# Rows of the twelve small experts gathered as halves of 2 KB into 128 partitions instead of 4 KB into 64

## The reference

```python
probs = jax.nn.softmax(jnp.dot(t, w_router).astype(jnp.float32), axis=-1)
...
h = jax.nn.silu(jnp.einsum("td,edf->tef", t, w_gate)) * jnp.einsum("td,edf->tef", t, w_up)
h = h * gates.astype(h.dtype)[..., None]
return jnp.einsum("tef,efd->td", h, w_down).reshape(B, L, D)
```

## Time and profile before

| | us |
|---|---|
| median of 3 runs | 646.52 (644.9 to 649.55) |
| span of the profiled execution | 643.7 |
| end of the last weight load in it | 613.9 |

### The profile page before, as it was taken

One profiled execution on the slowest core, in us unless ns is written; L12 is line 12 of the kernel. 1 busy time (PEld: TensorE's weight loads), 2 busy tenths in 40 slices (PEclk: granted clock), 3 DMA queues, 4 the chain that ended last, 5 costly groups with the idle time before them and its releaser, 6 DMA issues.

```text
span 643.7 us, 13218 instructions
## 1 busy us (share of the span) xinstructions
PE 562.1 (87%) x5746; PEld 369.7 (57%) x5746; DVE 245.1 (38%) x532; ACT 138.8 (22%) x265; POOL 66.0 (10%) x99
## 2 busy tenths in 40 slices
PE   2789999999999899879998899999997667688664
PEld 0475553566675655764465799998554434354332
DVE  2562457986854844631076821111110000001125
ACT  1240444423216710210034021001010000000012
POOL 1039000000004000002011010000010000100131
PEclk9898999999999999989999999999999988999968
DMA  8989920113030560999949899999999999999962
GB/s 271 392 299 370 347 104 28 63 69 131 1 130 9 208 252 1 339 330 245 400 159 381 322 326 390 386 384 395 363 389 392 391 387 394 392 408 408 356 227 98
DMA packets 80139, 175.98 MB, mean 273 GB/s; under 512 B 6504, under 2 KB 11631, under 8 KB 79695
## 3 DMA queue, kind: packets, MB, share of 16 engines
q1 hardware_dynamic: 65808, 149.02, 63.4%
q0 software_dynamic: 5920, 18.36, 8.1%
q10 hardware_dynamic: 8351, 7.73, 3.7%
HBM read 162.62 MB, written 12.47 MB: 272 GB/s over the span
## 4 chain that ended last, share of the span: by engine, by line
PE 24%; SPq 21%; DMA 4%; DVE 4%; issue 2%; ACT 0%; DVEq 0%
SPq L1155 9%; PE psum L927 5%; PE psum L825 5%; DMA slot<-in_w_down 4%; PE psum L924 4%; SPq L1168 3%; SPq L1184 2%; PE psum L935 2%; SPq L1225 2%; PE psum L832 2%; SPq L1172 2%; SPq L1181 1%; PE psum L841 1%; PE psum L1100 1%; PE psum L485 1%
## 5 line engine op out<-in xcount | busy, mean ns | idle before, releaser
L573 PE MATMUL psum<-hT,slot 128*128 128x384 f32 x304 | 100.8, 489 | 0.0
L935 PE MATMUL psum<-slot,xeTa 128*32 128x256 f32 x1152 | 69.2, 394 | 18.4 <-DMA slot<-in_w_gate 9.3
L573 PEld LDWEIGHTS psum<-hT,slot 128*128 128x128 f32 x304 | 56.9, 190 | 38.2
L935 PEld LDWEIGHTS psum<-slot,xeTa 128*32 128x32 f32 x1152 | 42.1, 113 | 44.7 <-issue 15.1
L582 PE MATMUL psum<-slot,hT 128*128 128x512 f32 x96 | 42.3, 595 | 1.2 <-DMA slot<-in_w_in 1.2
L935 PE MATMUL psum<-slot,heT 128*32 128x256 f32 x576 | 35.4, 401 | 8.6 <-DMA slot<-in_w_down 8.5
L1680 ACT ACTIVATE he<-psum 128x256 f32<-128x256 f32 (+1 forms) x16 | 6.6, 411 | 141.5 <-PE psum L935 113.0
L2363 DVE TENSOR_TENSOR he<-he,psum 128x256 f32<-128x256 f32 (+1 forms) x16 | 7.3, 454 | 73.0 <-PE psum L935 55.2
L2367 DVE COPY heT<-psum 128x256 f32<-128x256 f32 (+1 forms) x16 | 7.3, 458 | 70.8 <-PE psum L955 70.8
L924 PE MATMUL psum<-slot,xeTa 128*32 128x384 f32 x288 | 32.8, 487 | 0.3 <-issue 0.3
L927 PE MATMUL psum<-slot,xeTa 128*32 128x128 f32 x288 | 33.0, 273 | 0.0
(11 more groups left out here) (476 smaller groups left out, 912.1 us busy)
## 6 DMA issues: line engine op xcount, KB each, us to landing
slot<-in_w_ada SPq DMA_DIRECT2D x12, 2048.0 KB, 13.0
slot<-in_w_gate SPq DMA_DIRECT2D x12, 2048.0 KB, 17.5
slot<-in_w_up SPq DMA_DIRECT2D x12, 2048.0 KB, 18.3
slot<-in_w_down SPq DMA_DIRECT2D x12, 2048.0 KB, 19.5
slot<-in_w_in SPq DMA_DIRECT2D x7, 2048.0 KB, 11.3
const<-in_w_gate SPq DMA_DIRECT2D x4, 1792.0 KB
y_rows<-T POOLq DMA_DIRECT2D x11, 384.0 KB, 15.4
slot<-in_w_out SPq DMA_DIRECT2D x2, 2048.0 KB, 15.6
```

The costliest lines, as they stand in the source:

```text
L573: last = mm(o[:, 0:TOK], w[:, kt, tile(i)], hT[:, kt, :], start=(kt == 0), stop=(kt == KT - 1))
L935: last = mm(psum[32 * c:32 * c + 32, bank, 0:HALF], x(k, c % 2), w(k)[:, c // 2 * HALF:c // 2 * HALF + HALF], start=(k == 0), stop=(k == t ...
```

## The change

For the small experts the source of the gather is seen as 768 rows of 2 KB. Partition p below 64 fetches the first half of token row p, partition p from 64 on the second half of token row p - 64. Four transposes of 128 by 128 then fill the same bank of PSUM; block order in `xeTs` becomes 0, 4, 1, 5, 2, 6, 3, 7, and `up` reads it by that order. The doubled lists are made by one matmul with a new constant `twice` at the start of `expert(2)` on PE, and by an addition of 1 for the upper 64 partitions on DVE ahead of its work for expert 2. POOL waits for them ahead of the gather of n = 4 (before, it had them together with the list of n = 2). The two new constants, 129 columns, stand ahead of `dft_ctx` in `const`, and move all that lies behind them.

```diff
     put("triu", (p[:, None] < p[None]).astype(float))
+    put("twice", 2.0 * (p[:, None] == p[None] % SMALL))
+    put("upper", (p >= SMALL).astype(float)[:, None])
...
                 if small(n):
-                    for kt in range(KT):
-                        c = kt * SMALL
-                        last = tr(psum[:, 0, c:c + SMALL], src[0:SMALL, tile(kt)], ident[0:SMALL, 0:SMALL])
+                    for kt in range(KT // 2):
+                        last = tr(psum[:, 0, tile(kt)], src[:, tile(kt)], ident)
                     return last
...
                 if small(n):
-                    return packed_small(bank, lambda k, g: xeTs[p][:, k, 32 * g:32 * g + 32], lambda k: w[k], KT)
+                    return packed_small(bank, lambda k, g: xeTs[p][:, 2 * (k % 4) + k // 4, 32 * g:32 * g + 32],
+                                        lambda k: w[k], KT)
...
                 w = weights(n, 1)
+                if n == 2:
+                    pe.wait_ge(s["lists"], 1)
+                    mm(psum[:, 7, 32:32 + E - NBIG], C("twice"), OV[:, 10, NBIG:E], start=True, stop=True,
+                       skip_group_check=True).then_inc(s["sel_used"], 1)
...
                     if n + 1 == E - 1:
-                        pe.wait_ge(s["lists"], 2)
+                        pe.wait_ge(s["lists"], 3)
...
                 elif n == 2:
                     pool.wait_ge(s["lists"], 1)
+                elif n == NBIG:
+                    pool.wait_ge(s["lists"], 2)
...
-                m = SMALL if small(n) else ROWS
-                g.indirect_dma_start(out=xe[n % 2][0:m, :], out_offset=None, in_=A["h2_rows"],
-                                     in_offset=bass.IndirectOffsetOnAxis(ap=lst[0:m, n:n + 1], axis=0)
+                if small(n):
+                    to, of, by = xe[n % 2][:, 0:CW], A["h2_rows"].rearrange("t (h c) -> (t h) c", h=2), lst[:, n:n + 1]
+                else:
+                    to, of, by = xe[n % 2][0:ROWS, :], A["h2_rows"], lst[0:ROWS, n:n + 1]
+                g.indirect_dma_start(out=to, out_offset=None, in_=of, in_offset=bass.IndirectOffsetOnAxis(ap=by, axis=0)
                                      ).then_inc(s[f"xe{n % 2}"], 16)
...
-            v.tensor_copy(lst[:, 2:E], OV[:, 10, 2:E]).then_inc(s["lists"], 1)
+            v.tensor_copy(lst[:, 2:NBIG], OV[:, 10, 2:NBIG]).then_inc(s["lists"], 1)
...
-            def experts(it, first, last_pair=False):
+            def experts(it, first, last_pair=False, halves=False):
                 for p in range(2):
                     n = 2 * it + p
+                    if halves and p == 0:
+                        dve.wait_ge(s["sel_used"], NT + 1)
+                        v.tensor_scalar(lst[:, NBIG:E], psum[:, 7, 32:32 + E - NBIG], C("upper"), None, ALU.add
+                                        ).then_inc(s["lists"], 1)
...
-            experts(1, False)
+            experts(1, False, halves=True)
...
-            dve.wait_ge(s["sel_used"], NT + 1)
+            dve.wait_ge(s["sel_used"], NT + 2)
```

## The result

| | before | after |
|---|---|---|
| median of the runs, us | 647.06 (644.9 to 649.55, 4 runs) | 637.1 (636.43 to 638.13, 4 runs) |
| ratio, 95% interval | | 0.9865 [0.9828, 0.9901] |
| span of the profiled execution, us | 643.7 | 636.3 |
| last weight load issued and landed, us | 586.35, 613.9 | 578.02, 604.97 |

The change makes the kernel 1.35% faster, about 8.7 us by the ratio (6.4 to 11.1 us by its interval). The direction and the mechanism hold; the size does not.

A forecast was written before the change was run, and what follows sets the result against it. The DMA engines, not PE, were taken to bound the end of the experts. Terms -5.5 + 0.5 + 0 + 0 + 0.1 + 0.2 = -4.7 us gave a span of 639.0, a median of 641.8 us, range 638.5 to 648.0.

The forecast's parts named there:

- What bounds the kernel: End of the experts: set by the DMA engines, all 16 busy; PE time is not scarce; last weight load lands at 613.9.
- The loss: Behind each small gather the DMA rate drops from 404 to 347 GB/s: 0.64 us each, 7.6 us for twelve.
- half-rate reasoning: Small gather into partitions 0 to 63: at 202 GB/s per half it needs 1.30 us, 0.65 us more.
- Step 1: Small gathers into 128 partitions: 0.18 us of loss stays in each, gain 0.46 each, 5.5 us for twelve.
- Step 2: Twice the packets in the small gathers, on the DMA path: costs 0.04 us each, 0.5 us for twelve.
- Step 3: Four transposes instead of eight on PE: 0.69 us against 0.71, worth nothing on the time.
- Step 4: Late lists and POOL's wait for them: gather of n = 4 issued at 406.4, 2.7 us of cover, costs nothing.
- Step 5: Moved constants: longer load of `const` costs 0.1 us, gate matrix's new destination 0.2 us (bounds nothing and 4.6).
- Rival A: Small gathers: the loss goes altogether, being a matter of which half of the partitions is written; 639.6 us, chance 0.25.
- B: Small gathers: the loss stays, coming from fetching rows by a list in whatever partitions; 647.3 us, chance 0.20.
- C: Small gathers: the loss grows with the number of packets, holding up weight packets; 655 us, chance 0.08.
- D: Loads into `const`: packets to the moved destination take longer; gain gone at 4.7 us, or 657 us; chance 0.05.

The follow-up runs named there:

- e4_no_gather: Kernel before with the twelve small experts' gathers left out, a plain load of 1 KB in place of each: ratio 0.9755 to the kernel before.
- e8_eight: Changed kernel with eight products of 64 columns in place of the four transposes of 128: 638.04 us, ratio 0.9864 to the kernel before.
- e2_low: Control for e1_middle: same matmuls, constant and late lists, but the 64 whole rows land in partitions 0 to 63: ratio 0.9996 to the kernel before.
- e7_const_end: Changed kernel with its two new constants at the end of their table: 636.72 us, ratio 0.9849 to the kernel before.
- e1_middle: Kernel before with the 64 whole rows gathered into partitions 32 to 95, turned by selection matmuls, lists made late: ratio 0.9881.
- e3_halves_low: Kernel before with rows cut in 2 KB halves, two gathers of 64 halves, both into partitions 0 to 63: ratio 1.0022.
- e10_two_pieces: As e1_middle, but two gathers of 32 whole rows, into partitions 0 to 31 and 64 to 95: ratio 1.0005 to the kernel before.
- e6_spread4: As e1_middle, but four gathers of 16 whole rows, from partitions 0, 16, 64 and 80 on: 665.84 us, ratio 1.0306 to the kernel before.
- e12_quarters: Changed kernel with each small expert's rows in two gathers of 128 quarters of 1 KB into all 128 partitions: ratio 0.9917 to the kernel before.

## Why the prediction was wrong

**What bounds the kernel: right.** The DMA engines set the end: they finish 8.9 us earlier, and the slower tail takes 1.5 us of that back. The strip was read too evenly, though: DMA shows 8 and not 9 in slice 22, and PE has two slices of 8 among its 6 and 7 behind 480 us. The reading does not hang on it. PE is busy 11.60 of 16.00 us from 496 to 512 us, where it was 10.68, and waits for weights in the rest.

**The loss: right, a little small.** 12 * 0.64 = 7.6 us was called all that the change can win. The stretches of 4.5 us give 54 * (1 - 347/405.8) = 7.8 us with the rates of the two traces, the account with e4_no_gather 8.0. The half-rate reasoning (12 * 0.65 = 7.8 us) fits all three.

**Step 1: wrong, and it is the main term.** This is the step that failed. It took -5.5 us where -7.8 was measured, because it left a rest of 0.18 us of the loss in each gather where the rates show none. The residual of 0.18 us came from the closing gather, whose packets take 189 ns against 160 ns undisturbed, and by that ratio a 128-partition gather would have kept over half of the loss. In the kernel after, the small gather's own 64 packets take 10.6 us, 165 ns each with its 16 small ones counted to them. That is nearly the undisturbed time. So the 189 ns belonged to the tail and not to the form of the gather; what makes them long there was not tried. The row was the only one with 128 partitions, but not from the same situation.

**Step 2: wrong.** +0.5 us was for twice the packets; there are as many as before, 80140 against 80139. There was a row to doubt it by: nothing in the earlier trace rows says that one piece of the list is one packet, since 80 packets stood for 64 rows.

**Step 3: right.** Nothing that can be measured on the time, as e8_eight shows. Four transposes take 0.60 us, where 0.69 was worked out and eight took 0.71. All engines of the kernel after in order of time, around 416 us:

```profile
416.58 0.60 PE L946 MATMUL psum<-const,xe 128*128 128x128 f32 x4
```

**Step 4: right.** The gathers of n = 4 and 5 were put at 406.4 and 407.6. POOL, kernel after, in order of time, answers to the earlier trace rows:

```profile
406.00 0.99 POOL L1365 DMA_INDIRECT xe<-h_rows,lst  x1 [32.30 <-DVE lst L2372]
407.30 0.97 POOL L1365 DMA_INDIRECT xe<-h_rows,lst  x1 [0.30 <-issue]
```

PE turned the rows of n = 4 at 416.58, as before at 416.28, without a stop. e2_low has the same late lists at a ratio of 0.9996.

**Step 5: no cost is seen.** +0.3 us was taken. The loads into `const` run at 396 and 397 GB/s after, 389 before, and at 393 from 509.5 to 514 us in e7_const_end, which has the old destination. So the rates show no cost; the time of e7_const_end is too coarse to tell 0.3 us from nothing.

**The sum.** With -7.8, 0, 0, 0 and 0 it would have been 638.7 us. The median is 637.1, the ratio gives 637.8 (635.4 to 640.1). In the pair of traces the last load lands at 604.97 (near 609 was forecast), 8.9 us earlier, of which 0.4 was there before the first small gather and 0.6 is the load itself (26.95 against 27.53 us). These are of the size of the scatter between executions. That leaves nothing over that the runs could put a name to.

**The rivals and the range.** Rival A, the loss goes altogether, is what happened, in its reason too: it was given 0.25. What was held against it was the 96-row gathers, with a loss of 0.76 us each where halves explain 0.32. That number came from one stretch of one execution, and it is a poor one: the same stretch, 376 to 382.5, with the same code behind it, shows 310 before, 333 after, 301 in e7_const_end and 280 in e8_eight. It still loses more than halves explain in all of them, and why stays open; but it is no ground to expect a rest of the loss in the small gathers. B fell with the rates of 406. C fell with e1_middle, which has 80 packets a gather as before and no loss; the change itself does not test C, since its packets did not become more. D fell with the 396 and 397 GB/s of the loads into `const` (under 350 would have shown it) and with e7_const_end. The low end of the range was 1 us below rival A, and A had been charged with the 0.5 and 0.3 us of steps 2 and 5 as if these were sure, though step 5 itself had nothing as a bound and no row showed a cost for step 2. With them at nothing, A is at 638.8, and a margin below it of half the spread of the runs (4.7 us over the three of before) in place of the 1 us would have taken 637.1 in.

## What to carry to other kernels

When the DMA engines bound a kernel and the rate dips while their share stays at 1.0, look at which partitions the small transfers beside the stream are written to. One gather of 262 KB into partitions 0 to 63 halved the rate of all transfers together while it lasted, and put into 32 to 95 or into all 128 it cost only its bytes. The balance had to hold within each gather, because the gathers of POOL's queue were served one after the other (two valleys in e3_halves_low and e10_two_pieces, four in e6_spread4), so prefer one wide gather to several narrow ones. And when a cause is supported by a number that fits (0.65 against 0.64 us), a doubt that rests on a single short stretch should first be tested on how much that stretch scatters.

## What was not expected of the hardware

- A gather of 128 pieces of 2 KB is counted in as many packets as one of 64 pieces of 4 KB: 80 for 262 KB (80140 packets in all against 80139). Two gathers of 64 pieces of 2 KB have 96 (e3_halves_low), two of 128 pieces of 1 KB also 96 (e12_quarters).
- Gathers of 16 rows are dear. Four of them in the place of one of 64 rows made the kernel 3.1 to 3.5% slower, with a lowest 0.3 us slice of 137 GB/s in the mean of nine gathers, and moments with no DMA at work.
- A destination that is a multiple of 4 bytes but not of 32 within a partition did not slow 1.8 MB loads: 396 to 397 GB/s, where a multiple of 32 has 389 (before) and 393 (e7_const_end).
